# Differential attention in plain float32: projections moved inside the softmax steps

## The reference

```python
q, k, v = split(adaln(x) @ w_qkv)             # latent q, k get rotary positions
s0, s1  = q0 @ k0.T / 8, q1 @ k1.T / 8        # latent: 1024 own keys + 128 cached; context: 128 own keys
a = softmax(s0) - lam * softmax(s1)
o = a @ v                                     # then a norm per head and  o @ w_o
modulation = silu(cond) @ w_mod + b_mod       # shifts, scales and gates of both layers
```

## Time and profile before

| | |
|---|---|
| median of 3 runs | 3845.32 us (3844.67 to 3847.4) |
| span of the profiled execution | 3838.2 us |
| setup, until the first projection starts | 81.6 us |
| attention, from there to the last product with V | 1019.3 us |
| from there to the end of the last output projection product | 166.7 us |
| busy share of the span: PE, DVE, ACT, POOL | 87%, 48%, 20%, 22% |

### The profile page before, as it was taken

How to read it: one execution, slowest core, us unless ns; L and a number is a source line. 1 busy time by engine, 2 the same in 40 slices (tenths; PEclk the granted TensorE clock), 3 DMA queues, 4 the chain that set the end, 5 groups by cost and what they waited for, 6 DMA issues and landing times. The chain is left out here.

```text
span 3838.2 us, 61763 instructions
## 1 busy us (share of the span) xinstructions
PE 3328.2 (87%) x24360; PEld 3170.1 (83%) x24360; DVE 1857.8 (48%) x2724; ACT 760.3 (20%) x1770; POOL 863.6 (22%) x722
## 2 busy tenths in 40 slices
PE   5778877887779499999999999634999999999995
PEld 2778777886767399999999999523999999999995
DVE  4877687768756633232332323478332332323323
ACT  3334442443342000101001010211001001010011
POOL 2764466436501000000100001151000101001011
PEclk8899989988989699999999999766999999999997
DMA  5222112211123388786887867125886887868873
GB/s 190 58 69 64 53 54 73 65 49 54 57 97 130 135 306 280 244 295 234 296 280 244 293 234 265 56 77 182 276 294 233 296 272 253 293 234 295 273 252 123
DMA packets 409424, 722.27 MB, mean 188 GB/s; under 512 B 16737, under 2 KB 320514, under 8 KB 409378
## 3 DMA queue, kind: packets, MB, share of 16 engines
q1 hardware_dynamic: 388770, 669.12, 50.3%
q0 software_dynamic: 11616, 38.94, 4.0%
q10 hardware_dynamic: 8992, 13.63, 1.2%
HBM read 673.40 MB, written 48.23 MB: 188 GB/s over the span
## 5 line engine op out<-in xcount | busy, mean ns | idle before, releaser
L1470 PE MATMUL bank<-ex_xT,ring 128*128 128x144 f32 x11264 | 1389.1, 286 | 5.6 <-issue 2.8
L1470 PEld LDWEIGHTS bank<-ex_xT,ring 128*128 128x128 f32 x11264 | 1385.4, 190 | 6.4 <-issue 5.8
L1487 PE MATMUL bank<-ex_hid,ring 128*128 128x144 f32 x5632 | 698.5, 287 | 0.0
L1487 PEld LDWEIGHTS bank<-ex_hid,ring 128*128 128x128 f32 x5632 | 691.6, 190 | 0.9
L1426 POOL DMA_INDIRECT xres_lat<-ex_ye,ex_si x32 | 52.0, 1625 | 1747.8 <-ACT ex_ye L1524 1747.8
L1571 DVE TENSOR_SCALAR ex_yeC<-bank,valC 16x512 f32<-16x512 f32 x64 | 44.7, 734 | 668.2 <-PE bank L1500 668.2
L1559 DVE TENSOR_SCALAR ex_t<-ex_ge 128x432 f32<-128x432 f32 (+1 forms) x128 | 46.9, 366 | 662.3 <-ACT ex_ge L1510 662.3
L1560 DVE RECIPROCAL ex_t<-ex_t 128x432 f32<-128x432 f32 (+1 forms) x128 | 336.4, 2628 | 4.5
L1510 ACT ACTIVATE ex_ge<-bank 128x432 f32<-128x432 f32 (+1 forms) x128 | 64.0, 500 | 1305.6 <-PE bank L1470 1305.6
L1518 ACT ACTIVATE ex_yT<-bank,modc 128x128 f32<-128x128 f32 x256 | 95.3, 372 | 767.6 <-PE bank L1487 767.6
L894 DVE TENSOR_REDUCE nm<-bank 128x1 f32<-128x1152 f32 x144 | 176.6, 1234 | 119.4 <-PE bank L661 119.4
(11 more groups left out here) (224 smaller groups left out, 3995.1 us busy)
## 6 DMA issues: line engine op xcount, KB each, us to landing
ring<-in_expert_w_gate SPq DMA_DIRECT2D x96, 1536.0 KB, 8.6
ring<-in_expert_w_up SPq DMA_DIRECT2D x96, 1536.0 KB, 12.3
ring<-in_expert_w_down SPq DMA_DIRECT2D x96, 1536.0 KB, 12.1
ring<-in_expert_w_gate SPq DMA_DIRECT2D x32, 1024.0 KB
ring<-in_expert_w_up SPq DMA_DIRECT2D x32, 1024.0 KB, 8.6
ring<-in_expert_w_down SPq DMA_DIRECT2D x32, 1024.0 KB, 18.4
wmB<-in_w_mod SPq DMA_DIRECT2D x64, 384.0 KB, 3.3
wraw<-in_attn_wqkv SPq DMA_DIRECT2D x64, 192.0 KB, 2.9
```

Source lines behind the costliest of these rows:

```text
L1470: last = nc.tensor.matmul(bank[:, banks[j % 2], f * CAP:(f + 1) * CAP], wv[:, c, f * P:(f + 1) * P], xT[:, c], start=(c == 0), stop=(c == ...
L1487: last = nc.tensor.matmul(bank[:, YB[m // 3], (m % 3) * CAP:(m % 3 + 1) * CAP], wv[:, q, m * P:(m + 1) * P], hid[:, f], start=(f == 0), st ...
```

## The change

- **float32.** All splits go. `hT`, `wh`, `qT`, `kT`, `oT` and `wo` are float32. A tile's projection is 8 products of 384 columns, a score block one product with 64 rows, the output projection 16 products per tile. Tokens leave setup in one pass each, even groups on VectorE, odd groups on ScalarE.
- **Projections in the softmax steps.** Heads and tiles form one list of 72 steps k. Head 0 is projected first (9 tiles); step k then also projects tile k + 9, behind its own scores. The last 9 steps have no projection. Buffers of q, k, V and weights become double. All attention code is written out without a loop.
- **Scores one half-head at a time.** In a step the three blocks of half 0 are issued, then the three of half 1, each half with its own semaphore.
- **Order.** Step k: scores(k), projection(k + 9), transposes of a(k - 1), transposes of q and k of tile k + 8, `sums` in a head's last step, products with V of k - 1. The three groups of transposes write the banks of half 0 (waiting for its exponential), the q and k transposes a bank of half 1.
- **Modulation.** The columns of both layers form one row of 1280 per head and chunk. ScalarE multiplies (`products`, 2 instructions of 1280 columns per step, not in a head's last step), GpSimd adds (2 instructions), VectorE does none of it.
- **Transfers.** The weights of heads 0 and 1 are loaded in setup, later ones two heads ahead. The rotary tables go through SyncE's queue, ahead of the cached keys, whose transpose now stands ahead of the first projection. `wo` is loaded whole (4 MB) once the last projection is done. The ring of expert weights may load 6 instead of 5 slots early.

```diff
-RING_EARLY = (5, 6)
+RING_EARLY = (6, 6)
...
+        for h in range(2):
+            load_qkv_weights(sp, h)
...
+        def hT_out(n):
+            c, t0, nt, cond = hT_of(n)
+            act.wait_ge(xT_mm, n + 1)
+            nc.scalar.activation(hT[:, c, t0 * P:(t0 + nt) * P], bank[:, n % 8, 0:nt * P], ACT.Identity,
+                                 bias=modc[:, SHIFT1 * DC + c, cond:cond + 1],
+                                 scale=gains[:, 0, c, cond:cond + 1]).then_inc(hT_ok[1], 1)
...
-        for n in range(DC):
-            high_part(n)
+        act.wait_ge(gains_ok, 2)
+        for n in range(1, 3 * DC, 2):
+            hT_out(n)
...
+        for n in range(0, 3 * DC, 2):
+            c, t0, nt, cond = hT_of(n)
+            dve.wait_ge(xT_mm, n + 1)
+            nc.vector.tensor_scalar(hT[:, c, t0 * P:(t0 + nt) * P], bank[:, n % 8, 0:nt * P],
+                                    gains[:, 0, c, cond:cond + 1], modc[:, SHIFT1 * DC + c, cond:cond + 1],
+                                    ALU.mult, ALU.add).then_inc(hT_ok[0], 1)
...
+    def load_cache(h):
+        if h >= 2:
+            sp.wait_ge(S["kcT_mm"], h - 1)
+            sp.wait_ge(S["pv_mm"], TT * (h - 1))
+        sp.dma_start(kc[:, h % 2], kcd[:, h * VD:(h + 1) * VD]).then_inc(kc_in[h % 2], 16)
+        sp.dma_start(V[:, h % 2, LT], vcd[:, h * VD:(h + 1) * VD]).then_inc(S["vc_in"], 16)
...
+    def load_wm(h, c):
+        i = DC * h + c
+        if i >= 2:
+            sp.wait_ge(S["prod_ok"], 2 * (i - 1))
+        sp.dma_start(wm[:, i % 2, 0:MA], wmodA[:, c, h * MA:(h + 1) * MA]).then_inc(wm_in[i % 2], 16)
+        sp.dma_start(wm[:, i % 2, MA:MW], wmodB[:, c, h * MB:(h + 1) * MB]).then_inc(wm_in[i % 2], 16)
...
+    sp.dma_start(ctab[:], a["rope_cos"].rearrange("(t p) n -> p t n", p=P)).then_inc(S["tab_in"], 16)
+    sp.dma_start(stab[:], a["rope_sin"].rearrange("(t p) n -> p t n", p=P)).then_inc(S["tab_in"], 16)
+    load_cache(0)
+    load_cache(1)
+    store_kv(0)
+    for h in range(H):
+        for c in range(DC):
+            load_wm(h, c)
+            if c == 1:
+                if h + 2 < H:
+                    sp.wait_ge(S["qkv_mm"], TT * (h + 1))
+                    load_qkv_weights(sp, h + 2)
+                if h:
+                    store_kv(h)
+                    if h + 1 < H:
+                        load_cache(h + 1)
+            if c == 3 and h:
+                store_o(h - 1)
+    sp.wait_ge(S["qkv_mm"], STEPS)
+    sp.dma_start(wo[:], a["attn_wo"][0].rearrange("(h p) d -> p h d", p=P)).then_inc(wo_in, 16)
     store_o(H - 1)
...
-    with pool.Fori(0, H - 1) as h:
-        modulate(h)
-        pool.wait_ge(S["qkv_mm"], TT * h + TT)
-        for i in range(4):
-            split(i, 64 * h + 96 + 32 * (i // 2), 4 * h + 5 + i)
-    modulate(H - 1)
+    for h in range(H):
+        for c in range(1, DC):
+            pool.wait_ge(S["prod_ok"], 2 * (DC * h + c) + 2)
+            if c > 1:
+                pool.wait_ge(S["acc_ok"], 2 * ((DC - 1) * h + c - 1))
+            for cond in range(2):
+                nc.gpsimd.tensor_tensor(acc[:, cond], acc[:, cond], prod[:, cond], ALU.add
+                                        ).then_inc(S["acc_ok"], 1)
...
+    def qkv(g):
+        h, t = g // TT, g % TT
+        if t == 0:
+            pe.wait_ge(w_in[h % 2], 48 * (h // 2 + 1))
+        if g < TT:
+            if g >= 2:
+                pe.wait_ge(S["v_done"], g - 1)
+        else:
+            pe.wait_ge(S["v_done"], g)
+        for c in range(DC):
+            last = nc.tensor.matmul(bank[:, qkv_bank(g), 0:3 * VD], hT[:, c, t * P:(t + 1) * P], wh[:, h % 2, c],
+                                    start=(c == 0), stop=(c == DC - 1))
...
+    def scores(k):
...
+            pe.wait_ge(S["PT_ok"], groups_before(k - 1))
+        if k:
+            pe.wait_ge(S["qk_ok"], min(k + 8, STEPS))
+        blocks = [(b, 384 * b, 384) for b in range(3)] if n < LAST else [(0, KEYS, N_CTX)]
+        last = [None, None]
         for s in range(2):
+            for b, k0, width in blocks:
+                last[s] = nc.tensor.matmul(bank[:, 3 * s + b, 0:width],
+                                           qT[s * HD:(s + 1) * HD, h % 2, n * P:(n + 1) * P],
+                                           kT[s * HD:(s + 1) * HD, h % 2, k0:k0 + width], start=True, stop=True)
         for s in range(2):
+            last[s].then_inc(S_mm[s], 1)
...
+    def turn_a(k):
+        n = k % TT
+        pe.wait_ge(S["a_done"], k + 1)
+        if k + 1 < STEPS:
+            pe.wait_ge(exp_done[0], k + 2)
+        for i, (j0, j1) in enumerate(((0, 4), (4, 8), (8, 9)) if n < LAST else ((0, 1),)):
...
+    turn_cache(0)
+    for g in range(TT):
+        qkv(g)
+        if g:
+            turn_qk(g - 1)
+    for k in range(STEPS + 1):
+        h, n = k // TT, k % TT
+        if k < STEPS:
+            scores(k)
+        if k + TT < STEPS:
+            qkv(k + TT)
+        if k:
+            turn_a(k - 1)
+        if k < STEPS:
+            pe.wait_ge(exp_done[1], k + 1)
+            if k + LT < STEPS:
+                turn_qk(k + LT)
+            if n == 4 and h + 1 < H:
+                turn_cache(h + 1)
+            if n == LAST:
+                sums(h)
+        if k:
+            times_v(k - 1)
...
+    def products(h, c):
+        i = DC * h + c
+        act.wait_ge(wm_in[i % 2], 32 * (i // 2 + 1))
+        if c == 0:
+            if h:
+                act.wait_ge(S["sums_mm"], h)
+        else:
+            act.wait_ge(S["acc_ok"], 2 * ((DC - 1) * h + c - 1))
+        for cond in range(2):
+            dst = acc[:, cond] if c == 0 else prod[:, cond]
+            nc.scalar.activation(dst, wm[:, i % 2], ACT.Copy, scale=silu[:, cond, c:c + 1]).then_inc(S["prod_ok"], 1)
...
+            qk_out(g - 1)
+    for k in range(STEPS + 1):
+        h, n = k // TT, k % TT
+        if k < STEPS:
+            exp(k, 0)
+            exp(k, 1)
+        if k:
+            aT_out(k - 1)
+        if k + LT < STEPS:
+            qk_out(k + LT)
+        if k < STEPS and n == 4 and h + 1 < H:
+            cache_out(h + 1)
+        if k + TT < STEPS:
+            values(k + TT)
+        if k < STEPS and n < DC:
+            products(h, n)
+        if k:
+            o_out_of(k - 1)
...
+    for g in range(TT):
+        rotate(g)
+    for k in range(STEPS):
+        h, n = k // TT, k % TT
+        row_max(k, 0)
+        row_max(k, 1)
+        difference(k)
+        if k + TT < STEPS:
+            rotate(k + TT)
+        if n == LAST:
+            modulation(h)
...
+        pe.wait_ge(S["oT_ok"], t + 1)
+        if t == 0:
+            pe.wait_ge(wo_in, 16)
         for c in range(H):
-            if t == 0:
-                pe.wait_ge(S["wo_lo"], c + 1)
-            for k, (x, y) in enumerate(((oTh, woh), (oTh, wol), (oTl, woh))):
-                for b in range(2):
-                    last = nc.tensor.matmul(bank[:, b0 + b, :], x[:, t % 2, c], y[:, c, b * 512:(b + 1) * 512],
-                                            start=(c == 0 and k == 0), stop=(c == H - 1 and k == 2))
+            for b in range(2):
+                last = nc.tensor.matmul(bank[:, b0 + b, :], oT[:, t % 2, c], wo[:, c, b * 512:(b + 1) * 512],
+                                        start=(c == 0), stop=(c == H - 1))
...
-    for i in range(H):
-        act.wait_ge(wo_in[i], 16)
-        nc.scalar.activation(woh[:, i], woraw[raw_of(i)], ACT.Copy).then_inc(S["wo_hi"], 1)
...
-    oT_low(0)
-    for i in range(H):
-        dve.wait_ge(S["wo_hi"], i + 1)
-        nc.vector.tensor_tensor(wol[:, i], woraw[raw_of(i)], woh[:, i].bitcast(F32), ALU.subtract
-                                ).then_inc(S["wo_lo"], 1)
...
-        if attn and s + 1 < TT:
-            oT_low(s + 1)
...
-hTh = nc.alloc_sbuf_tensor_at("hTh", [P, DC, N_TOK], F32R, offset=persistent_end)
-hTl = nc.alloc_sbuf_tensor_at("hTl", [P, DC, N_TOK], F32R, offset=persistent_end + 4 * DC * N_TOK)
-setup_and_norm(hTh, hTl)
-attention(hTh, hTl, persistent_end + 2 * 4 * DC * N_TOK)
+setup_and_norm()
+attention(wh_end)
```

More of the change, by code:

```diff
@@ L356, in _ @@
                                                        1.0, colsA[:, 96:96 + DC], ALU.add, ALU.mult
[L357 to L381, removed]
@@ new lines, in attention @@
+                mx_done = [sem(st, f"at_mx_done{s}") for s in range(2)]
+                exp_done = [sem(st, f"at_exp_done{s}") for s in range(2)]
+                kc_in = [sem(st, f"at_kc_in{i}") for i in range(2)]
+                wm_in = [sem(st, f"at_wm_in{i}") for i in range(2)]
+                o_out = [sem(st, f"at_o_out{i}") for i in range(2)]
+                block = st.enter_context(nc.Block())
+                QKV_BANK, PV_BANK, TQK_BANK, SIDE_BANK = 6, 7, 4, 5
+                SUMS = 2 * MW // P
@@ new lines, in turn_qk @@
+                    def turn_qk(g):
+                        pe.wait_ge(S["rot_done"], g + 1)
+                        b = tqk_bank(g)
+                        if 4 <= g < LAST:
```

(34 more changed lines are left out.)

603 lines of the change are left out of this document (179 added, 424 removed).

## The result

The changed kernel takes **3724.28 us**, median of 4 runs (3722.64 to 3724.94); the kernel before takes 3846.36 beside it (4 runs, 3844.67 to 3852.04). The ratio is 0.9676, 95% interval 0.9662 to 0.9690: 122 us less, where 72 less was forecast. The sign came out as worked out, and so, within 1.5 us, did every changed stage but one, the seven heads; the time lies 49 us under the forecast and 16 under the lower end of the range.

What follows compares the result with a forecast made beforehand. The prediction saw projections bound by a chain through VectorE, not TensorE's speed. Its terms, -90.8 + 40.5 - 16.2 - 13.6 + 8 = -72.1, gave 3773 us from a median of 3845.3, range 3740 to 3835.

Steps and rivals of the forecast that it cites:

- the seven heads: Attention with projections inside the softmax steps: 115 us a head, 805 instead of 895.8 us in all, -90.8.
- the scores' term: Scores in a softmax step: 12 records of 384 columns at 0.323 us, 3.9 of a 12.5 us step.
- A rule against it: Switches between 64 and 128 rows, 0 to 14 us, against overlap of one record per step, up to 21; taken as 0.
- rival B: Scores in the softmax steps: the halves overlap at their border, 3752 us in all; chance 0.12.
- last head: Softmax of head 7 without projections to cover its chain: 98 us instead of 57.5, +40.5.
- context step: A head's last step: 16.0 us, with a wait for the adds until 9.3, then 4.6 for `sums` and 2.0 for V.
- Rival C: Smaller gain from switches, slow adds and first output projection tiles: about 3806 us, or 3815 with late copies; chance 0.08.
- Rival E: Softmax steps: the projection does not cover the chain, a step takes 15.2 us, 3924 in all; chance 0.05.
- Rival D: TensorE's clock at 0.89 instead of 0.99 over 857 us: +96, 3869 us; decides from 0.91 in the steps; chance 0.11.
- Start: Setup and loads up to the first projection: at 65.4 instead of 81.6 us, -16.2.
- head 0: Head 0's projections, bare ahead of the softmax steps: 52.4 instead of 66.0 us, -13.6.
- output projection: Stage after attention: 17.6 us a tile instead of 15.4, less some savings in the first tiles; net +8.

Runs made afterwards that it cites:

- e8_full_rows: The changed kernel with both halves' scores taken over all 128 rows of q and k instead of 64 each; 3763.58 us.
- e4_own_phase: The changed kernel with each head's projections taken out of the softmax steps and run between two heads; 4028.65 us, ratio 1.0474.
- e6_wide_sums: The changed kernel with half-heads' scores issued in turn (3681.31 us), plus products of `sums` over 128 equal columns of ones instead of one; 3653.02 us.

## Why the prediction was wrong in its size

**The step that failed** is the scores' term, "scores 12 records x 0.323 = 3.9", with the correction weighed against it under "A rule against it". The records do cost 0.323 to 0.332 each. But the prediction bounded the overlap of the halves by "one record of overlap per step", at most 21 us (rival B), and set it to nothing. One record is what fits at the border if records begin in the order in which they are issued; they did not. Half 1 starts with three records of half 0 left, and the overlap measured 1.18 us a step, 66 in the 56 steps of the seven heads. The switches, bounded there at 0 to 14 us, cost 0.38 a step, 21 over 56. So the net is -0.8 a step where 0 was taken: e8_full_rows, which has neither effect, runs at 12.56 us a step and 3764 us. In the last head, where the steps wait for the chain, the net was no gain: it takes 98.7 us with both effects, and 96.7 in e8_full_rows.

The 41 us by which the seven heads beat their forecast: 49 big steps at 11.76 instead of 12.5 are -36; the 1% allowed for the clock in 805 was not needed in the big steps, -8; the seven short and seven context steps took 764.3 - 49 x 11.76 = 188 instead of 184, +4. The rest of the 49 us is 5 for the reference (an execution of before quicker than the median, which the prediction took for time around the span) and 3 for the small differences of the table.

**The range** was too narrow on its lower side for the same reason. Its lower end, 3740, lies 12 us under rival B, which is an overlap of one record, and no row of before had a product of 64 rows to bound it. The bound from the rows at hand would have been full overlap, 6 x 0.323 = 1.94 us a step: the prediction had the mechanism and chose its smallest dose.

The Trainium skill (TensorEngine Tiling (Array Packing), Key Properties) says that a change of mode drains TensorE and that different tiles work in parallel. The runs fit both: 0.19 us for a change (that it is a drain no run shows), and 1.18 (issued half after half) to 1.93 us a step (issued in turn) for the parallel part. The second outweighs the first here.

**What was right.** The projection hides the chain of a softmax step; e4_own_phase shows the price without it, 304 us. Rival C's smaller gain is out with the time itself. Rival E is out: PE has no gap ahead of the transposes in a big step. Rival D is out in the big steps, at a granted clock of 1.00; in the seven heads together it is 0.96, above the 0.91 at which it would have decided. Start, head 0, output projection and last head came within 1.5 us each. For the last head that is partly luck: its products with V began 0.7 us earlier in a step than forecast (6.84, not 7.5) and took 1.0 longer (3.3, not 2.25), at a granted clock of 0.77 instead of the 0.89 assumed. In e8_full_rows, without the overlap, the same head ran at 0.89 and took 96.7. The context step is another cancelling pair: 2 us of wait that did not come, 3 of clock that did; e6_wide_sums puts this clock at 28 us in the whole kernel, 24 of it in the seven heads.

**Open**: why half 1 starts with three records of half 0 left, and why spreading `sums` among V's products does not keep the clock while making them wide does. The runs show that it is so, not what counts.

## What to carry to other kernels

When a product uses half of the rows, look at when the records of the two halves start, and issue the halves in turn: issued one after the other they overlapped by three records, in turn by all, 43 us here. When a mechanism has no row to size it, take its full size as the end of the range, not one unit of it. And read the granted clock beside the busy share: a stretch can be 100% busy and at half clock, and cheap extra columns or a few idle products (28 and 8 us here) can be worth more than the instructions cost.

## What the runs showed of the hardware that was not expected

- Products on rows 0 to 63 and 64 to 127 ran side by side, and not in the order of issue: half 1's first record began at 235.69 us, before the last three of half 0 (236.00 to 236.65) that stand ahead of it. Three were left with records of 384 columns and of 192 alike.
- A change between 64 and 128 rows took 0.19 us (12.94 against 12.56 a step, two changes each).
- During 40 records of one column, back to back, the granted clock fell to 0.50 (1.2 GHz) and stayed there for 6.8 us, with PE busy to 100% in the profile; the same 40 over 128 columns took 4.6 us and left it at 1.00 (2.4 GHz).
